# Two-layer decoder step: the norm boundaries around both MLPs, with the squares summed by TensorE and the first four tiles multiplied in three passes

## The reference, cut to what matters

```python
def rmsnorm(x, w):
    xf = x.astype(jnp.float32)
    y = xf * lax.rsqrt(jnp.mean(xf * xf, axis=-1, keepdims=True) + RMS_EPS)
    return (y * w.astype(jnp.float32)).astype(x.dtype)

yp = yp + rmsnorm(mp, norm_mix_post[l])
yp = yp + rmsnorm(sq_relu_mlp(rmsnorm(yp, norm_mlp_pre[l]), mlp_w1[l], mlp_w2[l]), norm_mlp_post[l])
```

## Time and profile before

| | |
|---|---|
| time, median of 3 runs | 3476.92 us (3473.77 to 3477.48) |
| the profiled execution: its own time | 3472.24 us |
| the profiled execution: its span | 3470.5 us, 47931 instructions |
| PE busy | 2876.5 us (83%) |
| PEld busy | 2587.0 us (75%) |
| DVE busy | 1375.0 us (40%) |
| ACT busy | 891.0 us (26%) |
| POOL busy | 993.9 us (29%) |
| mean granted clock of TensorE | 0.868 of full speed |

### The profile page before, as it was taken

How to read it: one execution, slowest core, us unless ns; L and a number is a source line. 1 busy time by engine, 2 the same in 40 slices (tenths; PEclk the granted TensorE clock), 3 DMA queues, 4 the chain that set the end, 5 groups by cost and what they waited for, 6 DMA issues and landing times. The chain is left out here.

```text
span 3470.5 us, 47931 instructions
## 1 busy us (share of the span) xinstructions
PE 2876.5 (83%) x19979; PEld 2587.0 (75%) x19979; DVE 1375.0 (40%) x2639; ACT 891.0 (26%) x1572; POOL 993.9 (29%) x459
## 2 busy tenths in 40 slices
PE   6766578777678799997797877887999878799998
PEld 5643477754458799997786767876998667799998
DVE  6664320048733332225274436444002544332224
ACT  4211121024302421224232124112221224432112
POOL 2220122024302443334323212331323431443331
PEclk9866799579958899998898779887998888899998
DMA  4100333533011122222220002001232006222221
GB/s 139 52 0 25 91 58 95 105 120 154 13 37 49 49 86 86 76 84 77 65 75 13 27 26 63 15 26 38 84 95 99 1 25 188 66 74 86 86 78 59
DMA packets 217605, 232.89 MB, mean 67 GB/s; under 512 B 40972, under 2 KB 186700, under 8 KB 216782
## 3 DMA queue, kind: packets, MB, share of 16 engines
q1 hardware_dynamic: 202686, 225.20, 21.2%
q10 hardware_dynamic: 14704, 4.63, 0.6%
HBM read 207.86 MB, written 48.35 MB: 74 GB/s over the span
## 5 line engine op out<-in xcount | busy, mean ns | idle before, releaser
L270 POOL TENSOR_TENSOR WRr<-WR,WH 128x2048 fp32r<-128x2048 f32 (+3 forms) x98 | 443.1, 4522 | 960.2 <-ACT WH L258 960.2
L2025 PE MATMUL PS<-HHr,WRr 128*128 128x288 f32 x1152 | 344.1, 299 | 0.0
L410 PE MATMUL PS<-HHr,WH 128*128 128x288 f32 (+1 forms) x928 | 279.0, 301 | 52.0 <-PEq L96 52.0
L410 PE MATMUL PS<-YTr,WRr 128*128 128x288 f32 x1024 | 303.8, 297 | 0.0
L410 PE MATMUL PS<-YTr,lt_WX 128*128 128x288 f32 x1408 | 281.8, 295 | 0.3 <-POOL WRr L270 0.3
L258 ACT CAST WH<-WR 128x2048 fp32r<-128x2048 f32 (+3 forms) x98 | 180.4, 1841 | 387.9 <-DMA WR<-in_mlp_w 193.1
L410 PE MATMUL PS<-HHr,WRr 128*128 128x288 f32 (+1 forms) x928 | 278.4, 300 | 0.0
L410 PE MATMUL PS<-HTr,WH 128*128 128x288 f32 (+1 forms) x928 | 278.3, 300 | 0.0
L2025 PE MATMUL PS<-HHr,WH 128*128 128x288 f32 x768 | 228.7, 298 | 9.4 <-POOL HTr L2013 8.7
L410 PE MATMUL PS<-WH,HHr 128*128 128x256 f32 (+3 forms) x760 | 219.6, 289 | 19.1 <-PEq L96 19.1
L270 POOL TENSOR_TENSOR WRr<-WR,lt_WX 128x2048 fp32r<-128x2048 f32 x35 | 162.2, 4633 | 230.8 <-ACT lt_WX L258 230.8
(11 more groups left out here) (639 smaller groups left out, 6650.4 us busy)
## 6 DMA issues: line engine op xcount, KB each, us to landing
WR<-in_mlp_w SPq DMA_DIRECT2D x64, 1024.0 KB, 5.3
WR<-in_cd_w_in SPq DMA_DIRECT2D x34, 1024.0 KB, 5.4
out_dil_s<-in_cache_dil_kv SPq DMA_DIRECT2D x2, 7936.0 KB
WR<-in_ab_w_in SPq DMA_DIRECT2D x10, 1024.0 KB, 5.3
past_rows<-in_cache_nsa_kv SPq DMA_DIRECT2D x16, 256.0 KB, 3.5
YT<-in_state_ssm ACTq DMA_DIRECT2D x16, 256.0 KB, 4.5
out_ssm_s<-YT SPq DMA_DIRECT2D x16, 256.0 KB
WR<-in_ab_w_in SPq DMA_DIRECT2D x16, 256.0 KB, 4.3
```

The costliest lines, as they stand in the source:

```text
L270: pool.tensor_tensor(K.WRr[:, n % RING, 0:used], K.WR[:, n % RING, 0:used], high_slot(K, i, used).bitcast(F32), ALU.subtract).then_inc(K.l ...
L410: last = pe.matmul(out, a, b, start=(n == 0), stop=(n == 3 * len(terms) - 1))
L2025: last = pe.matmul(out, a[:, k, c], h[:, k, x], start=(n == 0), stop=(n == 3 * KT - 1))
```

## The change

For half 0, GpSimd adds only the squares of the tiles 0 to 3; TensorE sums that and then the squares of the tiles 4 to 7 one by one, five float32 products into one bank. For half 1 GpSimd adds nothing: TensorE takes all eight squares one by one (`chain_ones3`), four after the second pass and four in the middle of the third. The second norm's sums get banks of their own (`bank2`). The second root of half 0 and the first root of half 1 are made together, logarithm, logarithm, exponential, exponential (`chain_rms23`); in `A` this now stands before the cast of the second MLP chunk, and two relus have moved ahead of `chain_high` of half 1. The first four tiles of each half are made in three passes over the four tiles (`quarter_products`): wh·hh, then wl·hh, then wh·hl; `K.mm` is raised only in the third. On GpSimd the subtraction of the second chunk follows three additions in place of seven.

```diff
--- before.py
+++ after.py
@@ -281,6 +281,15 @@
     return high_slot(K, i, kt * cols).rearrange("p (k n) -> p k n", k=kt), slot(K.WRr, n, RING, kt, cols)
+def high_wait(K, pe, n):
+    kt, cols = K.chunks[n][:2]
+    i = K.split_at[n]
+    pe.wait_ge(K.hi, i + 1)
+    return high_slot(K, i, kt * cols).rearrange("p (k n) -> p k n", k=kt)
 def inv_rms(act, K, ss, n, summed, count, link):
     act.wait_ge(summed, count)
...
@@ -1929,10 +1938,30 @@
     pe.matmul(K.PS[:, C.bank + b, 0:HALF], K.ones[:], K.SS1[:, b, :], start=True, stop=True).then_inc(C.ones, 1)
-def chain_ones2(K, pe, C, b):
-    pe.wait_ge(C.ss2, 7 * (b + 1))
-    pe.matmul(K.PS[:, C.bank + b, 0:HALF], K.ones[:], K.SS2[:, b, :], start=True, stop=True).then_inc(C.ones, 1)
+def chain_ones2(K, pe, C):
+    out = K.PS[:, C.bank2, 0:HALF]
+    pe.wait_ge(C.ss2, 3)
+    pe.matmul(out, K.ones[:], K.SS2[:], start=True, stop=False)
+    for k in range(4, KT):
+        pe.wait_ge(C.sq2, k + 1)
+        last = pe.matmul(out, K.ones[:], K.SQ2[:, k % 4, :], start=False, stop=(k == KT - 1))
+    last.then_inc(C.ones, 1)
+def chain_ones3(K, pe, C, ks):
+    for k in ks:
+        pe.wait_ge(C.sq2, KT + k + 1)
+        pe.matmul(K.PS[:, C.bank2 + 1, 0:HALF], K.ones[:], K.SQ2[:, k % 4, :], start=(k == 0), stop=(k == KT - 1),
+                  skip_group_check=True).then_inc(C.sq2_used, 1)
+def chain_log(K, act, rs, C):
+    act.activation(rs, rs, ACT.Ln, scale=1.0 / D, bias=K.eps[:]).then_inc(C.link, 1)
 def chain_rms(K, act, C, b, n):
@@ -1940,8 +1969,32 @@
     rs = K.PS[:, C.bank + b, 0:HALF]
     act.wait_ge(C.ones, n)
-    act.activation(rs, rs, ACT.Ln, scale=1.0 / D, bias=K.eps[:]).then_inc(C.link, 1)
+    chain_log(K, act, rs, C)
     act.wait_ge(C.link, n)
+    act.activation(rs, rs, ACT.Exp, scale=-0.5).then_inc(C.rs, 1)
+def chain_rms23(K, act, C):
+    r2, r3 = K.PS[:, C.bank2, 0:HALF], K.PS[:, C.bank + 1, 0:HALF]
+    act.wait_ge(C.ones, 2)
+    chain_log(K, act, r2, C)
+    act.wait_ge(C.ones, 3)
+    chain_log(K, act, r3, C)
+    act.wait_ge(C.link, 2)
+    act.activation(r2, r2, ACT.Exp, scale=-0.5).then_inc(C.rs, 1)
+    act.wait_ge(C.link, 3)
+    act.activation(r3, r3, ACT.Exp, scale=-0.5).then_inc(C.rs, 1)
+def chain_rms4(K, act, C):
+    rs = K.PS[:, C.bank2 + 1, 0:HALF]
+    act.wait_ge(C.sq2_used, KT)
+    chain_log(K, act, rs, C)
+    act.wait_ge(C.link, 4)
     act.activation(rs, rs, ACT.Exp, scale=-0.5).then_inc(C.rs, 1)
@@ -1965,23 +2018,25 @@
     for k in ks:
         i = KT * b + k
         act.wait_ge(C.x_new, i + 1)
-        if i >= 4:
-            j, kk = (i - 4) // KT, (i - 4) % KT
-            act.wait_ge(C.ss2, 7 * j + max(kk, 1))
+        if b == 0 and k >= 4:
+            act.wait_ge(C.ss2, max(k - 4, 1))
+        if b == 1 and k < 4:
+            act.wait_ge(C.ones, 2)
+        if b == 1 and k >= 4:
+            act.wait_ge(C.sq2_used, k - 3)
         act.activation(K.SQ2[:, i % 4, :], K.XT[:, k, half_of(b)], ACT.Square).then_inc(C.sq2, 1)
-def chain_add(K, pool, C, b):
-    for k in range(1, KT):
-        i = KT * b + k
-        pool.wait_ge(C.sq2, i + 1)
+def chain_add(K, pool, C):
+    for k in range(1, 4):
+        pool.wait_ge(C.sq2, k + 1)
         if k == 1:
-            pool.tensor_tensor(K.SS2[:, b, :], K.SQ2[:, (i - 1) % 4, :], K.SQ2[:, i % 4, :], ALU.add).then_inc(C.ss2, 1)
+            pool.tensor_tensor(K.SS2[:], K.SQ2[:, 0, :], K.SQ2[:, 1, :], ALU.add).then_inc(C.ss2, 1)
         else:
-            pool.wait_ge(C.ss2, 7 * b + k - 1)
-            pool.tensor_tensor(K.SS2[:, b, :], K.SS2[:, b, :], K.SQ2[:, i % 4, :], ALU.add).then_inc(C.ss2, 1)
+            pool.wait_ge(C.ss2, k - 1)
+            pool.tensor_tensor(K.SS2[:], K.SS2[:], K.SQ2[:, k, :], ALU.add).then_inc(C.ss2, 1)
 def chain_h(K, dve, C, b):
@@ -1991,7 +2046,7 @@
     dve.wait_ge(C.rs, RS2[b])
     dve.wait_ge(C.x_new, KT * (b + 1))
     for k in range(KT):
-        dve.scalar_tensor_tensor(K.HT[:, k, x], K.XT[:, k, x], K.normT[:, C.pre, k:k + 1], K.PS[:, C.bank + b, 0:HALF],
+        dve.scalar_tensor_tensor(K.HT[:, k, x], K.XT[:, k, x], K.normT[:, C.pre, k:k + 1], K.PS[:, C.bank2 + b, 0:HALF],
                                  ALU.mult, ALU.mult).then_inc(C.h, 1)
@@ -2013,18 +2068,37 @@
         pool.tensor_tensor(K.HTr[:, k, x], K.HT[:, k, x], K.HH[:, k, x].bitcast(F32), ALU.subtract).then_inc(C.hl, 1)
-def half_product(K, pe, out, wh, wl, c, b, C=None):
+def half_product(K, pe, out, wh, wl, c, b):
     x = half_of(b)
     n = 0
     for k in range(KT):
-        if C is not None:
-            pe.wait_ge(C.hl, KT * b + k + 1)
         for a, h in ((wh, K.HH), (wh, K.HTr), (wl, K.HH)):
             last = pe.matmul(out, a[:, k, c], h[:, k, x], start=(n == 0), stop=(n == 3 * KT - 1))
             n += 1
     return last
+def quarter_products(K, pe, C, b, first, banks, free, done, aside=None):
+    x = half_of(b)
+    for step, h in enumerate((K.HH, K.HH, K.HTr)):
+        for j in range(4):
+            w = split_wait(K, pe, first + j // 2)[1] if step == 1 else high_wait(K, pe, first + j // 2)
+            c = slice((j % 2) * P, (j % 2 + 1) * P)
+            if step == 0:
+                free(j)
+            for k in range(KT):
+                if j == 0 and step != 1:
+                    pe.wait_ge(C.hl if step else C.hh, KT * b + k + 1)
+                last = pe.matmul(K.PS[:, banks + j, 0:HALF], w[:, k, c], h[:, k, x], start=(step == 0 and k == 0),
+                                 stop=(step == 2 and k == KT - 1), skip_group_check=True)
+            if step == 2:
+                last.then_inc(done, 1)
+            if aside is not None:
+                aside(step, j)
 def layer_tail(nc, K, layer, parts):
...
@@ -2138,17 +2212,18 @@
                                 last.then_inc(K.mm, 1)
                             if b == 1 and o == 6 and c == 0:
                                 chain_ones1(K, pe, A, 0, 8)
-                chain_ones2(K, pe, A, 0)
+                def other_half(C):
+                    def aside(step, j):
+                        if (step, j) == (1, 3):
+                            chain_ones3(K, pe, C, range(0, 4))
+                        if (step, j) == (2, 1):
+                            chain_ones3(K, pe, C, range(4, KT))
+                    return aside
+                chain_ones2(K, pe, A)
                 chain_ones1(K, pe, A, 1, 10)
-                Ws = [split_wait(K, pe, up0 + c) for c in range(2)]
-                for j, b in up_halves:
-                    if b:
-                        pe.wait_ge(relu_done, j + 1)
-                    wh, wl = Ws[j // 2]
-                    half_product(K, pe, K.PS[:, j, 0:HALF], wh, wl, slice((j % 2) * P, (j % 2 + 1) * P), b,
-                                 A if j == 0 else None).then_inc(K.mm, 1)
-                    if (j, b) == (2, 0):
-                        chain_ones2(K, pe, A, 1)
+                quarter_products(K, pe, A, 0, up0, 0, lambda j: None, K.mm, other_half(A))
+                quarter_products(K, pe, A, 1, up0, 0, lambda j: pe.wait_ge(relu_done, j + 1), K.mm)
                 def up(r):
                     for half in range(2):
@@ -2192,16 +2267,10 @@
                     if (o, b) == (1, 1):
                         chain_ones1(K, pe, Z, 0, KT)
                 if layer == 0:
-                    chain_ones2(K, pe, Z, 0)
+                    chain_ones2(K, pe, Z)
                     chain_ones1(K, pe, Z, 1, 2 * KT)
-                    Ws = [split_wait(K, pe, gz + c) for c in range(2)]
-                    for i, (j, b) in enumerate(up_halves):
-                        pe.wait_ge(acc_done, KT * LAST + 13 + i) if i < 4 else pe.wait_ge(z_out, i - 3)
-                        wh, wl = Ws[j // 2]
-                        half_product(K, pe, K.PS[:, 4 + i % 4, 0:HALF], wh, wl, slice((j % 2) * P, (j % 2 + 1) * P), b,
-                                     Z if j == 0 else None).then_inc(K.mm, 1)
-                        if (j, b) == (2, 0):
-                            chain_ones2(K, pe, Z, 1)
+                    quarter_products(K, pe, Z, 0, gz, 4, lambda j: pe.wait_ge(acc_done, KT * LAST + 13 + j), K.mm, other_half(Z))
+                    quarter_products(K, pe, Z, 1, gz, 4, lambda j: pe.wait_ge(z_out, j + 1), K.mm)
                     for j in range(4, KT):
                         if j % 2 == 0:
                             wh, wl = split_wait(K, pe, gz + j // 2)
@@ -2259,9 +2328,8 @@
                 piece(8)
                 chain_square(K, act, A, 0, range(4, 8))
                 piece(9)
+                chain_rms23(K, act, A)
                 split_high(K, act, up0 + 1)
-                chain_rms(K, act, A, 0, 2)
-                chain_rms(K, act, A, 1, 3)
                 chain_high(K, act, A, 0)
                 chain_square(K, act, A, 1, range(0, 8))
@@ -2271,10 +2339,10 @@
                 relu_half(0, 0)
                 relu_half(1, 0)
-                chain_rms(K, act, A, 1, 4)
-                chain_high(K, act, A, 1)
```

(39 more changed lines are left out.)

## The result

The changed kernel takes 3485.07 us (median of 8 runs, 3482.17 to 3488.24) against 3474.82 of the kernel before in the same comparison (8 runs): ratio 1.003, 95% interval 1.0019 to 1.0041. It is 10.3 us slower. I forecast 1.2 us faster, with a range that ended at 3482. Repeated later it gave 3481.99 against 3474.83 (1.0028, 1.0018 to 1.0038).

The account below looks back on a forecast made before the run. TensorE, busy 83%, was taken as the bound, so boundary shifts reach the end: -4.0 us for the first and third boundaries, +2.8 for the second, -1.2 in sum; 3475.7 rounded to 3476.0, range 3472 to 3480, with rivals 3468 to 3482.

Parts of the forecast that it names:

- Start of half 0 in `A`: First and third boundary: fewer GpSimd additions and two table loads fewer start the first product 4.2 us earlier.
- Half 0 in three passes: First and third boundary: passes run from 1192.2 to 1211.3 without waits; 3.4 us more ones work leaves 2.1 of 4.2.
- Half 1 in `A`: First and third boundary: PE restarts after 1.5 us idle; gain 2.6 or 1.3, taken as 2.0 us each.
- the clock term: Half 1 at the first and third boundary: a clock falling in the sparse stretch adds 1.3 us.
- `Z`: Second boundary: GpSimd's earlier subtraction holds VectorE, last square 3.7 us later; boundary ends 2.8 us later.
- Weights: Weight slot released 2.1 us before half 1's end, where it was 6.3; slack 2.7 us, so cost nothing.
- rival 2: Late slot release delays the weight chunk at three boundaries: 3478.4 us, or 3483.8 at worst; chance 0.12.
- rival 3: Batching logarithms and exponentials saves no table loads at three boundaries: +7.7 us, 3483.7; chance 0.06.
- Rival 4: Clock stays low under the sparse first pass, ones products run at 0.50: +14.6 us, 3490.6; chance 0.04.

Follow-up runs that it names:

- fillers: First and third boundary changed, plus products whose results go unused around half 1's first tile, against the kernel before: 3469.72 us against 3474.83 (0.9988).
- early sums: Whole change with GpSimd's subtraction late at the second boundary and half 1's squares summed earlier on TensorE, against the kernel before: 3468.81 us against 3475.69 (0.9978).
- `Z` alone: Only the second boundary changed, first and third as before, against the kernel before: 3474.88 us against 3475.68 (0.9998).
- batched roots: Kernel before with only logarithms together and exponentials together at all three boundaries: 3462.74 us against 3474.83 (0.9966); again 3462.61 against 3475.69 (0.9969).

## Why the prediction was wrong

**Start of half 0 in `A`: right.** Two table loads for four. At the third boundary it comes about 4 us earlier (said 4.2).

**Half 0 in three passes: right.** 19.2 us at the third boundary (said 19.1). Four ones products, each of two records, take 2.10 us in the stream (0.5 each, as priced), and nothing there is late.

**Half 1 in `A`: the restart right, the clock term mis-sized.** Idle 1.25 us (said 1.5), restart about 2 earlier as said. But I let a low clock cost 1.3 us; it cost 2.4, since the 24 products behind the sparse first tile were slow too (8.7 us for pass 1 where fillers make it 6.3), and it fell in 14 of the 16 such passes in the profiles of `A` without fillers and early sums, not in half. So `A` mostly gave -0.6 and +0.3 instead of -2.0 each. Only two profiled executions kept the clock at the first boundary, with -3.1. The failed step is this term, and with it the chance of one half that the clock falls.

**`Z`: the mechanism right, the size half.** The Trainium skill's rule ("SBUF — State Buffer", section "SBUF: two separate sides") held: 4.52 us for a held addition. The term of 2.8 measured 5.6 and 6.8, and 5.4 in both profiles without what lies ahead of the first changed instruction. In the first of them, with the offset of 3.8 taken out, the start was 0.3 later than before, not 0.6 earlier (0.9), and from the start to half 1's logarithm it was 18.5, not 17.4 (another 1.1): pass 1 took 8.3 us at a mean granted clock of 0.59. That makes 4.8; the other 0.6 stands behind the restart of half 1.

**Weights: right.** No wait for the second chunk in the round behind the four tiles; rival 2 didn't come. Nor did rival 3. Rival 4 neither: the eight ones products in half 0's passes ran at the upper clock (1.00); it was half 1's first pass that didn't.

**What no step and no rival had.** I priced added instructions by their time and untouched code at nothing. The 3.3 and 3.5 us in the dilated stage are what is left of 6.1 and 6.6 us of waits for instructions, which come with the program's length ahead of the stage, behind 2.7 us that a higher clock gave. Terms: -0.7, +6.8, +3.5 and -0.2 make +9.4 for the second profile of the changed kernel, +0.8 between 1240 and 1600, of which the rounds gave 2.9 back; its median was 7.2 slower, the first one's 10.3. With the clock of before at the start of that stage it would be the 2.7 more. The range, which ended at 3482, had room for none of this.

**What stays open.** Why executions of one program differ by up to 10 us ahead of the change, and why the rounds behind the second boundary gave back 0 in one profile and 2.9 in another. Of the 10.3 some 3 may be that. Why the refills come late, by full DMA engines or by the pace at which the stage uses up its instructions. Why `Z` alone isn't slower in the median, and where 4 to 5 of the 12 to 13 us of the batched roots come from.

## What to carry to other kernels

Test the parts of a bundle one by one: here one part (roots batched by table) was worth 12 to 13 us and the rest of the bundle ate it. When work moves onto the engine that sets the end, count where it stands in that engine's program, because all that waits for it inherits the products ahead of it; and when a gap is shortened but not closed, price the clock at its low level for the whole of the next pass. Where a stage fills the DMA queues and uses up instructions fast, some 60 to 100 instructions more anywhere ahead of it can move its time by several us, so compare that stage by itself before blaming the edit. And one profile can't price an edit of 1 us: an unchanged stretch differed by 1.4 and 2.7 us between executions by the clock alone.

## What was not expected of the hardware

- 100 instructions more in TensorE's program brought 5.5 to 7.4 us of waits into a stage with a DMA share of 1.06, and 60 more took them away again (7.4 and 0.6 us). These waits end 1.24 to 1.74 us after an instruction packet has landed.
- The batched roots gave 2.9, 2.4 and 2.8 us at the boundaries, near their two table loads (2.56 us each), but 12.1 and 13.1 us in the medians.
- 24 unused products ahead of and inside a sparse stretch of half 1 made its first pass 2.4 us shorter (6.3 for 8.7), by keeping the granted clock at its upper level.
